# Expert stage of a decoder layer: gathered rows turned by DVE instead of PE, weight rests written in place, a quarter of them by GpSimd

## What is computed

```python
x = x + mix
x = x + HierMoE(RMSNorm(x))      # top-1 of 4 groups, then top-2 of 8 experts
def expert_block(args):
    xb, e = args
    h = jax.nn.silu(xb @ w1[e]) * (xb @ w3[e])
    return h @ w2[e]
out = jnp.zeros((N + 1, D), jnp.float32).at[buf_tok].add(y * buf_gate[:, None])[:N]
```

## Time and profile before

| | us |
|---|---|
| three runs, median (lowest to highest) | 1178.31 (1177.29 to 1178.64) |
| the profiled execution | 1177.93 |
| its span, first to last instruction | 1175.9 |
| busy in the span: PE / DVE / ACT / POOL | 1109.1 / 885.2 / 730.2 / 138.1 |
| mean granted TensorE clock | 0.975 of full |

### The profile page before, as it was taken

How to read it: one execution, slowest core, us unless ns; L and a number is a source line. 1 busy time by engine, 2 the same in 40 slices (tenths; PEclk the granted TensorE clock), 3 DMA queues, 4 the chain that set the end, 5 groups by cost and what they waited for, 6 DMA issues and landing times. The chain is left out here.

```text
span 1175.9 us, 16929 instructions
## 1 busy us (share of the span) xinstructions
PE 1109.1 (94%) x5868; PEld 907.8 (77%) x5868; DVE 885.2 (75%) x1013; ACT 730.2 (62%) x914; POOL 138.1 (12%) x192
## 2 busy tenths in 40 slices
PE   8999999999999989997899999999999999999960
PEld 7887777777778758886688888888888888888840
DVE  4505757566475673568799999999999999999957
ACT  5423555656734482211688888888888888888840
POOL 1001010000000011001001101101101101111000
PEclk9999999999999999997999999999999999999995
DMA  7211010101011054003999999999999999999619
GB/s 224 51 35 38 19 37 19 36 19 37 18 36 37 4 215 193 36 37 116 375 426 422 383 401 384 388 390 381 387 388 388 383 385 375 387 380 386 241 67 383
DMA packets 59835, 261.90 MB, mean 223 GB/s; under 512 B 14224, under 2 KB 36240, under 8 KB 46608
## 3 DMA queue, kind: packets, MB, share of 16 engines
q1 hardware_dynamic: 48992, 240.32, 53.0%
q0 software_dynamic: 9216, 16.80, 3.7%
q10 hardware_dynamic: 1584, 4.20, 0.9%
HBM read 252.89 MB, written 25.17 MB: 236 GB/s over the span
## 5 line engine op out<-in xcount | busy, mean ns | idle before, releaser
L1138 DVE TENSOR_TENSOR e_lo<-W,e_hi 128x1024 fp32r<-128x1024 f32 x384 | 452.4, 1219 | 23.2 <-ACT e_hi L1132 20.3
L1132 ACT ACTIVATE e_hi<-W 128x1024 fp32r<-128x1024 f32 x384 | 403.4, 1060 | 94.2 <-PE ps L1103 92.6
L1101 PE MATMUL ps<-e_hi,xT_hi 128*128 128x512 f32 x512 | 203.3, 397 | 4.5 <-DVE e_lo L1138 3.5
L1103 PE MATMUL ps<-e_lo,xT_hi 128*128 128x512 f32 x512 | 200.5, 392 | 0.0
L1102 PE MATMUL ps<-e_hi,xT_lo 128*128 128x512 f32 x512 | 199.9, 390 | 0.0
L433 PE MATMUL ps<-xnT_hi,w_hi 128*128 128x512 f32 x320 | 128.6, 402 | 2.4 <-DVE y_mix L817 0.9
L851 DVE TENSOR_TENSOR_SCAN kept<-kept,start_at 128x1024 f32<-128x1024 f32 (+7 forms) x64 | 88.4, 1381 | 53.3 <-ACT kept L654 53.3
L433 PE MATMUL ps<-xnT_hi,w_lo 128*128 128x512 f32 x320 | 128.0, 400 | 0.0
L433 PE MATMUL ps<-xnT_lo,w_hi 128*128 128x512 f32 x320 | 124.9, 390 | 0.0
L1101 PEld LDWEIGHTS ps<-e_hi,xT_hi 128*128 128x128 f32 x512 | 96.8, 189 | 23.8 <-DVE e_lo L1138 3.7
L663 ACT ACTIVATE probsT<-ps 128x512 f32<-128x512 f32 (+3 forms) x96 | 43.6, 490 | 111.8 <-PE ps L482 111.6
(11 more groups left out here) (234 smaller groups left out, 1690.2 us busy)
## 6 DMA issues: line engine op xcount, KB each, us to landing
W<-in_w_dram SPq DMA_DIRECT2D x96, 2048.0 KB, 12.6
w_raw<-in_w_in_dram SPq DMA_DIRECT2D x20, 512.0 KB, 4.1
yy<-y_rows SPq DMA_DIRECT2D x7, 1024.0 KB, 11.9
xt<-in_x_dram SPq DMA_DIRECT2D x8, 512.0 KB, 3.8
w_out_raw<-in_w_out_dram SPq DMA_DIRECT2D x8, 512.0 KB, 6.9
xn_rows<-xn SPq DMA_DIRECT2D x8, 512.0 KB, 2.6
out_dram<-x ACTq DMA_DIRECT2D x7, 512.0 KB, 8.6
x<-in_x_dram SPq DMA_DIRECT2D x2, 1536.0 KB, 10.1
```

What stands on the lines that cost most here:

```text
L1101: pe.matmul(o, xs_hi[:, k], e_hi[:, p, cols], start=(k == 0), stop=False)
L1103: mm = pe.matmul(o, xs_hi[:, k], e_lo[:, p, cols], start=False, stop=(k == last))
L1132: act.activation(e_hi[:, p], flat[:, p * D:(p + 1) * D], ACT.Copy).then_inc(s["hi_made"], 1)
L1138: dve.tensor_tensor(e_lo[:, p], flat[:, p * D:(p + 1) * D], e_hi[:, p], ALU.subtract).then_inc(s["lo_made"], 1)
```

## The change

- The rows of an expert (from expert 2 on) are gathered in four parts: the index list `quarter_row` names quarters (1 KB) of rows, so that partition `32a+i` holds in its part `t` the quarter `a` of the row of slot `32t+i`. One DVE instruction (`dve_turn_quads`, a transpose in blocks of 32x32) then makes `xraw`, the turned rows, in SBUF. PE no longer turns them. ACT and DVE make `xT_hi` and `xT_lo` from `xraw`. `quarter_row` is made once, by four small matmuls with masks `pick` that POOL writes.
- The rest of a piece is written over the raw weights (`rest_of`), which leaves room for eight rounded pieces (`e_hi[0]`, `e_hi[1]`). ACT runs up to eight pieces ahead, and a weight buffer is loaded again when PE has used it (`freed`) and not when DVE has read it.
- Of the four rests of a matrix POOL makes the second (`POOL_PIECE = 1`, `pool_split`), DVE the other three (`dve_most`), from expert 1 on.
- The orders within a round are written anew.

```diff
-        e_hi = at("e_hi", 80, [P, PIECES, D], F32R)
-        e_lo = at("e_lo", 64, [P, PIECES, D], F32R)
+        e_hi = [at(f"e_hi{i}", kib, [P, PIECES, D], F32R) for i, kib in enumerate((80, 64))]
+        xraw = at("xraw", 160, [P, D])
...
         def used(pieces):
-            return pieces + PIECES
+            return pieces + 2 * PIECES
...
+        def dve_most(dve, part, name, b, half):
+            dve_split(dve, s_e, part[0], name, b, half, [p for p in range(PIECES) if p != POOL_PIECE])
+
+        def pool_split(pool, part, name, b, half):
+            p = POOL_PIECE
+            pool.wait_ge(s_e["hi_made"], part[0] + p + 1)
+            pool.tensor_tensor(piece(rest_of[name][b], p), piece(flat_of[name][b], p), e_hi[half][:, p], ALU.subtract).then_inc(lo_by_pool, 1)
...
+        def act_xT_quads(act, n):
+
+            act.wait_ge(s_e["turned"], n + 1)
+            act.wait_ge(s_e["freed"], used(up_part(n - 1)[0] + PIECES))
+            act.activation(xT_hi.rearrange("p k t -> p (k t)"), xraw, ACT.Copy).then_inc(s_e["xT_hi_made"], 1)
+
+        def dve_turn_quads(dve, n, b, gathered):
+
+            dve.wait_ge(s_e["gathered"][b], gathered)
+            dve.wait_ge(s_e["xT_made"], n)
+            dve.transpose(xraw.rearrange("p (k t i) -> p t k i", k=KT, t=QUADS),
+                          xg[b].rearrange("p (t i k) -> p t k i", t=QUADS, k=KT)).then_inc(s_e["turned"], 1)
+
+        def dve_xT_quads(dve, n):
+            dve.wait_ge(s_e["xT_hi_made"], n + 1)
+            dve.tensor_tensor(xT_lo.rearrange("p k t -> p (k t)"), xraw, xT_hi.rearrange("p k t -> p (k t)"),
+                              ALU.subtract).then_inc(s_e["xT_made"], 1)
...
+        def gather_quarters(pool, n, b, gathered, turned, indexed):
+
+            pool.wait_ge(s_e["gathered"][b], gathered)
+            pool.wait_ge(s_e["turned"], turned)
+            pool.tensor_copy(idx_token[b].unsqueeze(2), quarter_row[:, :, bass.ds(n, 1)]).then_inc(s_e["indexed"], 1)
+            pool.wait_ge(s_e["indexed"], indexed)
+            for t in range(QUADS):
+                start_step(pool)
+                pool.indirect_dma_start(out=xg[b][:, t * QCOLS:(t + 1) * QCOLS], out_offset=None, in_=xn2_quarters,
+                                        in_offset=bass.IndirectOffsetOnAxis(ap=idx_token[b][:, t:t + 1].bitcast(U32), axis=0),
+                                        bounds_check=QUADS * S - 1, oob_is_err=False).then_inc(s_e["gathered"][b], 16)
...
                 def load(w, wv, e, b, landed, n):
 
-                    sp.wait_ge(s_e["lo_made"], n + PIECES)
+                    sp.wait_ge(s_e["freed"], used(n + PIECES))
...
+                def round_of(e, b, i):
+
+                    splits_ahead(e, b)
+                    pool_scatter(pool, s_e, e - 2, b, i - 1, e - 2, 2 * e)
+                    split_down(e - 1, 1 - b)
+                    gather_quarters(pool, e + 3, 1 - b, 64 * (i + b) + 16, e + 2, 2 * e + 1)
...
+                def round_of(e, b):
+                    g_half, u_half, _ = halves_of(e, b)
+                    pe_gate(pe, s_e, e, gate_part(e), b, g_half)
+                    pe_turn_hid(pe, s_e, e - 1)
+                    pe_up(pe, s_e, e, up_part(e), b, u_half)
+                    pe_down(pe, s_e, e - 1, down_part(e - 1), 1 - b, 1 - b)
...
+                def round_of(e, b, i):
+                    g_half, u_half, _ = halves_of(e, b)
+                    dve_most(dve, gate_part(e), "W1", b, g_half)
+                    dve_hid(dve, s_e, e - 1, up_part(e - 1)[0])
+                    if isinstance(e, int) and e == 1:
+                        dve_xT(dve, s_e, 1)
                     else:
-                        dve_split(dve, s_e, gate_start(e), W1[b])
-                    dve_split(dve, s_e, up_start(e), W3[b])
...
+                        dve_xT_quads(dve, e)
+                    dve_most(dve, up_part(e), "W3", b, u_half)
+                    if i is not None:
+                        dve_turn_quads(dve, e + 1, 1 - b, 64 * i + 80)
+                    dve_most(dve, down_part(e - 1), "W2", 1 - b, 1 - b)
+                    dve_hidT(dve, s_e, e - 1)
```

More of the change, by code:

```diff
@@ L1078, in expert_sems, with piece, pe_turn_x @@
                 "scattered": [sem(f"{tag}_scattered{i}") for i in range(2)]}
+        POOL_PIECE = 1
+        flat_of = {"W1": [w.rearrange("p k f -> p (k f)") for w in W1], "W3": [w.rearrange("p k f -> p (k f)") for w in W3],
+                   "W2": [w.rearrange("p k f -> p (k f)") for w in W2]}
         def used(pieces):
-            return pieces + PIECES
-        def pe_turn_x(pe, s, n, b, rounds):
-            pe.wait_ge(s["gathered"][b], 16 * rounds)
+            return pieces + 2 * PIECES
+        def piece(t, p):
+            return t[:, p * D:(p + 1) * D]
+        def pe_turn_x(pe, s, n, b, gathered):
+            pe.wait_ge(s["gathered"][b], gathered)
             pe.wait_ge(s["xT_made"], n)
@@ L1091, in pe_turn_x, with wait_rest, pe_product @@
             mm.then_inc(s["turned"], 1)
-        def pe_product(pe, s, start, xs_hi, xs_lo, out, per_piece, last, pieces=range(PIECES)):
+        def wait_rest(pe, s, part, p):
+            start, lo, pool_lo = part
+            if pool_lo is None:
+                pe.wait_ge(s["lo_made"], lo + p + 1)
+            elif p == POOL_PIECE:
+                pe.wait_ge(lo_by_pool, pool_lo)
+            else:
+                pe.wait_ge(s["lo_made"], lo + (p if p > POOL_PIECE else p + 1))
+        def pe_product(pe, s, part, name, b, half, xs_hi, xs_lo, out, per_piece, last, pieces=range(PIECES)):
             for p in pieces:
-                pe.wait_ge(s["lo_made"], start + p + 1)
+                wait_rest(pe, s, part, p)
                 for j in range(D // BANK):
@@ new lines, in round_of @@
+                def round_of(e, b, i):
[3 more added lines that the diff above has]
+                    gather_quarters(pool, e + 3, 1 - b, 64 * (i + b) + 16, e + 2, 2 * e + 1)
+                splits_ahead(1, 1)
+                split_down(0, 0)
+                gather_quarters(pool, 4, 0, 80, 3, 3)
+                for e in range(2, 4):
+                    round_of(e, e % 2, e // 2)
@@ L1473, in _ @@
                 pe.matmul(ps[0:1, 3, 0:P], over_col, ident, start=True, stop=True).then_inc(list_turned, 1)
-                for i in range(14):
+                pe.wait_ge(picks_made, 2 * QUADS)
+                pe.wait_ge(tokens_made, 1)
+                for t in range(QUADS):
+                    mm = pe.matmul(ps[:, 6, t * NE:(t + 1) * NE], pick[:, t], token_f, start=True, stop=True)
+                mm.then_inc(tokens_made, 1)
+                for i in range(12):
                     pe.transpose(ps[:, 4, 0:P], ident, ident)
@@ L1484, in first_gate @@
                 def first_gate():
+                    gate = lambda pieces: pe_product(pe, s_e, gate_part(0), "W1", 0, 0, xT_hi, xT_lo, [ps[:, 2]], 2, KT - 1, pieces)
                     pe.wait_ge(half_lo_made, 1)
[L1486 removed]
+                    gate((0, 1))
                     pe.wait_ge(s_e["xT_made"], 1)
[L1488 to L1503 removed]
```

278 lines of the change are left out of this document (151 added, 127 removed).

## The result

| | before | after |
|---|---|---|
| median of the runs, us | 1178.5 (1177.3 to 1178.8) | 1306.6 (1303.3 to 1313.0) |
| profiled execution, its span, us | 1177.9, 1175.9 | 1303.3, 1301.5 |
| ratio of the times | | 1.109 [1.107, 1.112] |
| one expert round, us | 17.75 | 21.90 |

What follows compares the result with a forecast made beforehand. PE bound the kernel at 17.76 us a round; DVE would take over: 14.66 own work + 6.0 held - 1.77 covered = 18.89. Thirty rounds at 1.13 more, less 1.1, gave 1211 us; range 1152 to 1247.

Steps and rivals of the forecast that it cites:

- The mechanism: Expert rounds: POOL's SBUF reads and DVE instructions with two SBUF inputs exclude each other, DVE becomes the bound; chance 0.62.
- The transpose, 1.16: DVE's new 32x32-block transpose of 128x1024 each round: one rest's 1.16 us, between bounds 0.68 and 2.3.
- A POOL rest, 1.90 to 2.36, hold 2.0: Each of POOL's three subtractions a round takes 1.90 to 2.36 us and holds DVE 2.0, within 1.72 to 2.36.
- Cover 1.77: Per round, 1.77 of 6.0 us hold is hidden: W2 rest under the transpose (1.16), W1 rest beside `hid` (0.61).
- PE then waits about 2 us a round: With DVE the bound at 18.89 us a round, PE idles about 2 us in each, released by DVE.
- The range: Whole kernel: 1152 to 1247 us, taking in most of rival 1; the likeliest case's own range was 1186 to 1247.
- Rests in place, eight chunks, ACT, loads: nothing: ACT running eight chunks ahead costs nothing; weight loads starting at most 5.5 us later cost nothing.
- Round 1: 1.1 gained: Expert 1's gate product, waiting 3.53 us at 577.32, gains 1.1 us because W1's rests come before `xT_lo`.
- Rival 1: Expert rounds: faster, as POOL and DVE waits interlock and PE's 16.88 us bounds the round; 1150 at full size; chance 0.26.
- DMA bound of 17.46: Weight loads: DMA engines only 2% ahead of demand, alone allowing 17.46 us a round, 1168 in all.
- Rival 3: Expert rounds: much slower, POOL's queue of gathers, rests and waits is the bound at 20.7 us, 1266; chance 0.07.
- Rival 4: Gathers in quarters make 1 KB pieces that may crowd the queues and delay weights; adds nothing unless rival 1 holds.

Runs made afterwards that it cites:

- e5: Changed kernel with POOL writing zeros by memset where it subtracted for a rest, those products left out of the result; 1152.7 us, 0.979 of the kernel before.
- e6: Changed kernel with DVE's transpose reading its input in memory order instead of strided, x then wrongly ordered; 1282.0 us, 1.088 of the kernel before.
- e3: Changed kernel with one gather, PE turning x and DVE making all rests; rests in place and eight rounded chunks stay; 1179.8 us, 1.0015 of the kernel before.
- e4: Changed kernel with POOL's row scatter moved from behind the W1 and W3 rests to between them; 1266.5 us, 1.074 of the kernel before.
- e8: As e7, but POOL makes only the last chunk of W1 and W3, each started by DVE's rest ahead of it; 1204.5 us, 1.022 of the kernel before.
- e9: As e8, with two of the four gathers moved behind POOL's W1 rest; 1199.6 us, 1.0185 of the kernel before.
- e11: As e9, but with only one of the four gathers behind POOL's W1 rest; 1177.7 us, 0.9993 of the kernel before.
- e1: Changed kernel with DVE making all twelve rests and POOL none; four-part gathers, transpose and rests in place stay; 1209.3 us, 1.026 of the kernel before.
- e7: Changed kernel with the turned rows `xraw` in PSUM instead of SBUF; 1230.6 us, 1.045 of the kernel before.

## Why the prediction was right and wrong

- **The mechanism** (POOL rests and DVE instructions with two SBUF inputs exclude each other, DVE becomes the bound) was right, though DVE idles 1.15 us a round: e5 takes POOL's subtractions away and 154 us go. That PSUM readers and the transpose escape was right too; the transpose never exceeded 2.24 in the changed kernel. The direction was forecast with it.
- **The transpose, 1.16**: mis-sized, 2.04 a round. The bound of 2.3 contained it; the middle was chosen by the number of columns, without looking at the stride of the input (e6).
- **A POOL rest, 1.90 to 2.36, hold 2.0**: 2.41 alone, and the DVE rest behind takes 3.42 where 1.21 is bare, so a hold of 2.2: 0.2 too small, three times a round.
- **Cover 1.77**: this step failed. The prediction laid the W2 rest beneath the transpose and `hid` beside the W1 rest in every round. The W2 rest lies beneath the transpose in eight of the 30 rounds, those of the second kind; in the others (one more overlaps by half) it comes 0.3 to 1.5 us after the transpose has ended, as it waits 3.7 to 4.9 us for ACT:

```profile
871.77 2.07 DVE L1189 STREAM_TRANSPOSE xraw<-xg 128x1024 f32<-128x1024 f32 x1
875.25 2.40 POOL L1172 TENSOR_TENSOR W_rest<-W,e_hi 128x1024 fp32r<-128x1024 f32 x1 [4.76 <-ACT e_hi L1159]
...
894.24 2.21 DVE L1189 STREAM_TRANSPOSE xraw<-xg 128x1024 f32<-128x1024 f32 x1
894.12 2.47 POOL L1172 TENSOR_TENSOR W_rest<-W,e_hi 128x1024 fp32r<-128x1024 f32 x1
```

With holds of 2.2 the cover was 6.6 less 5.5, 1.1 a round. The prediction also put the W1 rest on one of DVE's rests and only the W3 rest on `xT_lo`; in 20 rounds both pass at once, on the instruction for which PE waits. Held were 5.5 a round, not 4.23.
- **"PE then waits about 2 us a round"**: for `xT_lo` alone it waits 3.0 (89.3 / 30), in one piece, and the chunks released late behind that wait, at half clock, cost DVE 1.15 us of idle a round. The prediction had no term for what a wait of PE gives back to DVE. The three misses, 0.7 us of own work, 1.3 held and 1.15 idle, make 18.9 into 22.0.
- **The range**: the bounds that the prediction gives for its terms (transpose 2.3, hold 2.36, no cover) add up to 22.9 a round, about 1330 us. The range stopped at 1247, because at its upper end only the hold (2.2) and `hid`'s cover move.
- **Rests in place, eight chunks, ACT, loads: nothing**: right, by e3 (0.15%).
- **Round 1: 1.1 gained**: the gate product of expert 1 does start earlier, at 576.11 in place of 577.32, but PE then waits 4.55 for `hidT_lo` at 593.98, and the `xT_lo` of expert 2 starts at 597.77, where it started at 593.52.
- **Rival 1**: its PE-bound size, 1150, is what e5 gives (1152.7, round 16.80 where 16.88 was worked out). Its DMA bound of 17.46 was wrong: the same queues carry a round in 16.80, so a share of 0.98 to 1.01 with landing times that hardly fall was a queue kept full, not a limit.
- **Rival 3** (POOL's queue as bound): no, POOL was busy 27 of 40 us, but its order matters: e4 differs from the changed kernel by nothing else, nor do e8, e9 and e11 from each other.
- **Rival 4**: nothing in e5, with the same 1 KB pieces.

## What to carry to other kernels

When work goes to GpSimd beside a full VectorE, count what each SBUF-reading GpSimd instruction holds and where in VectorE's order it falls; let a semaphore start it when VectorE turns to PSUM readers or a transpose that last as long, and keep the value that the waiting engine needs next in PSUM (76 us for one line here). Price a transpose by its stride. And add up what the move gives and takes: a rest given to GpSimd frees VectorE of 1.14 us and holds it for 2.2 where nothing covers it, so about half of the hold must be covered before it pays. e1, e8 and e11 show it. They have the same transpose; e1 gives GpSimd no rest and its round is 18.72. e8 gives it two, with 2.0 us held: 18.57, hardly a gain. e11 gives it the same two, with 1.1 held: 17.63.

## What the hardware showed beyond this

- GpSimd instructions that follow each other without a gap can all pass a waiting VectorE instruction: two rests and 6.2 us, four halves and 6.5, rest, copy and rest and 6.3 to 6.5. It goes the other way too: in e1 VectorE's four rests in a row passed a GpSimd copy (4.32 us in the median).
- The block transpose of 128x1024 f32 takes 1.23 us read in order and 2.17 at a stride of 32 bytes, from SBUF to SBUF; its output in PSUM changes little (2.24 in e7).
- A GpSimd memset of 128x1024 took 0.95 to 0.99 us in all 94 cases of e5, beside VectorE's two-input rests too, and lengthened none of them.
